# First layer of a two-block kernel: norm by tokens, split input projections, six modulation steps moved

## The chip, the cores and the metric

The program runs on one core of a Trainium2 chip. The metric is the time of one execution in microseconds on the device; lower is better. The core's engines run side by side, each through its own list of instructions, and meet at semaphores: TensorE (PE, its weight loads are shown apart as PEld), VectorE (DVE), ScalarE (ACT), GpSimd (POOL) and SyncE (SP), which issues nearly all large transfers. TensorE adds its results into 8 banks of PSUM.

## What is computed

Two blocks run one after the other on 256 tokens of width 1024, in fp32. The change touches only layer 0 of the first block:

```python
sh1_l, sc1_l, g1_l, sh2_l, sc2_l, g2_l = jnp.split(jax.nn.silu(c) @ ada_w[i] + ada_b[i], 6, axis=-1)
hl = modulate(rms_norm(xl, norm_mix[i]), sh1_l, sc1_l)      # h * (1 + scale) + shift
...  # hc the same way from xc = ctx and c_ctx, where a layer reads the context
yl, yc = even_mixer(hl, hc, ev_w_in[j], ...)                # layer 0
xl = xl + g1_l[:, None] * yl
hl2 = modulate(rms_norm(xl, norm_ffn[i]), sh2_l, sc2_l)
xl = xl + g2_l[:, None] * expert_choice_ffn(hl2, router[i], w_gate[i], w_up[i], w_down[i])
```

`ada_w` is 2 x 1024 x 6144: both layers take their shifts, scales and gates from a product of the condition vector with it. `even_mixer` projects both streams (`h @ w_in`: q, k, v, z, gates and the input of the pooling), runs q, k and v through a convolution of three taps and SiLU, normalizes q and k, runs a gated delta rule over chunks of 64 tokens in both directions (the context gives the start state), pools the pooling input in windows of 2, 4, 8 and 16 along rows of 64 tokens, and multiplies the sum by `w_out`. Then come 16 experts of width 512, each on the 32 tokens that it chooses. Layer 1 has a short convolution in place of the mixer and experts again. The second block isn't touched.

## The kernel before

`build` writes the program of every engine by hand, one function for each, so the order in the code is the order on the engine. PE fills banks in turn: `v_open`/`v_close` a bank of the four that DVE empties, `s_open`/`s_close` one of the four for ACT; on the other side `take` waits for the next filled bank and `drained` gives it back.

**Weights.** `stream` lists chunks of 2 MB (1024 rows by 512 columns). SP loads them in that order into `weight_ring`, four slots for the first 31 chunks; `free_slot` makes SP wait until the chunk that was in the slot has been used (`released`). The stream begins with four chunks of `ada_w`, five of `ev_w_in` (qkv in three, z, pool), the other twenty of `ada_w`, two of `ev_w_out`. Behind them come the experts' chunks of layer 0, in more slots.

**Modulation.** One chunk of `ada_w` is one step: `ada_turn` turns the copied result of the step before with four transposes (through `transposes`, L532) for DVE's `ada_bias`, which sums it and adds the bias; `ada_mm` multiplies the next chunk, 8 matmuls of 32 x 512 (L579), and ACT copies its bank in `ada_copy` (L1470). Each layer has 12 steps. Four come in the head, since the first norm needs them; the others are entries `"ada"` in the list of `mixer_steps`, by which PE, DVE, ACT and POOL all build the mixer. Its pieces there are the rows of decay (`rows`), products of keys, the inverse of each chunk's triangle by levels (`turn`, `grow`, `flip`), `solve` and `kdec` for each head, and `walk`, the pass over the chunks (`state`, `w`, `out`), once for each direction.

**Head.** PE transposes x and ctx (16 banks, L558 and L562), ACT squares the transposed form (L1455 and L1456), `norm_part` sums the squares over features with eight 512-wide matmuls against ones (L596), ACT and DVE make the reciprocal root, DVE scales (L1819, 16 operations of 256 columns) and ACT adds the shift (L1431).

**Projections.** `project` multiplies a chunk in plain fp32 (L636), four quarters of 128 output columns, each over 8 tiles of features. The first qkv chunk and z and pool have 256 columns (x alone), the other two qkv chunks 512 (x and ctx). Behind each quarter ACT copies the bank (L1506 for qkv) and DVE does the convolution. Between z and pool stand the gates' product (`l2_sum` and the gate matmuls, L671 and L678) and the gates' transposes. DVE pools a quarter as it comes (L1975 and the lines behind it), with reciprocal counts made there (L1985). ACT has the Ln/Exp pairs of the l2 norms (L1530, L1532) there.

**The split form.** The rest of the kernel multiplies in `product`: input and weights are each split into a high part (ACT's copy into a shorter type, L1395 for weights, in `high`) and the remainder (DVE's subtraction in `split`, through the helper L1816), and three matmuls (L652 to L654) go over each tile: high by high, low by high, high by low. There are two buffers for the parts of a quarter's weights; `high` waits for the quarter two back to be multiplied.

## Time and profile before

| | us |
|---|---|
| median of 3 runs | 1449.2 |
| lowest and highest | 1444.81 and 1453.25 |
| the profiled execution | 1447.19 |
| its span, first to last instruction | 1445.5 |
| TensorE busy (matmuls) in it | 1212.5 (84%) |
| VectorE, ScalarE, GpSimd busy | 583.4, 413.3, 78.1 |
| mean granted clock of TensorE | 0.928 |

The shares are averages over stages with different limits, so the stages have to be read one by one. PEclk and the clock are shares of TensorE's full speed. A matmul's row gives its duration from start to a modelled end; neighbouring ones overlap, so the distance between two starts is what one costs. "x16" is a run of sixteen instructions. "idle before <-releaser" tells how long the engine had stood idle and which work ended that.

### The profile page before, as it was taken

Reading aid. Unit: us, or ns where it says so; the run is one execution under the profiler, and the core shown is the slowest. Engines: PE = TensorE matmul, PEld = TensorE weight load, DVE = VectorE, ACT = ScalarE, POOL = GpSimd, SP = SyncE. Lnnn points to the kernel's source line nnn. Section 1 sums busy time; section 2 is a strip of 40 time slices with the busy share of each in tenths; the row PEclk is TensorE's granted clock in tenths of the full one; section 3 lists DMA queues with packets and bytes.
Section 4 is the critical chain, followed back from the end, with each engine's and each line's share of the span. In section 5 each row is a group of like instructions: output and inputs, shape, how many; then the busy total and the mean of one; then the engine's idle time right before and its main releaser. Section 6 shows DMA issues by size and latency. Waiting matters only on the chain.

```text
span 1445.5 us, 19111 instructions
## 1 busy us (share of the span) xinstructions
PE 1212.5 (84%) x8105; PEld 873.1 (60%) x8105; DVE 583.4 (40%) x1076; ACT 413.3 (29%) x751; POOL 78.1 (5%) x118
## 2 busy tenths in 40 slices
PE   5899889998986566589998655658899999999887
PEld 2646658785952122159986212115899878899756
DVE  1432684544530000036653000002796366545574
ACT  2323433222310000024332000001454555343562
POOL 4000023430000000000000000000000000010000
PEclk9999999999998788799999988888999999999998
DMA  8713374349589999993547999999243403444000
GB/s 300 292 58 117 127 249 150 117 165 378 203 323 409 409 409 409 409 385 118 186 183 298 410 409 409 409 409 391 94 166 129 147 29 117 175 142 173 36 1 30
DMA packets 125097, 338.63 MB, mean 234 GB/s; under 512 B 8657, under 2 KB 11590, under 8 KB 125014
## 3 DMA queue, kind: packets, MB, share of 16 engines
q1 hardware_dynamic: 117536, 334.51, 60.8%
q10 hardware_dynamic: 7478, 2.91, 0.8%
q8 instruction: 65, 1.06, 0.3%
q14 instruction: 18, 0.15, 0.0%
HBM read 336.35 MB, written 1.05 MB: 233 GB/s over the span
## 4 chain that ended last, share of the span: by engine, by line
PE 62%; DMA 20%; DVE 8%; SPq 6%; ACT 3%; issue 1%; ACTq 0%; DVEq 0%
PE bank L652 9%; PE bank L654 9%; PE bank L653 8%; DMA weight_ring<-in_w_up_dram 7%; PE bank L636 6%; SPq L1220 5%; PE bank L940 4%; DMA weight_ring<-in_w_gate_dram 3%; DVE arena L1816 3%; PE bank L579 2%; PE bank L1104 2%; PE bank L596 2%; DMA weight_ring<-in_w_down_dram 2%; DMA expert_slots<-in_w_down_dram 2%; DMA expert_slots<-in_w_up_dram 2%; SPq L1225 2%
## 5 line engine op out<-in xcount | busy, mean ns | idle before, releaser
L652 PE MATMUL bank<-input_high,weights_high 128*128 128x256 f32 (+1 forms) x992 | 291.7, 294 | 6.6 <-DVE input_low L1816 6.6
L654 PE MATMUL bank<-input_high,weights_low 128*128 128x256 f32 (+1 forms) x992 | 285.0, 287 | 0.0
L653 PE MATMUL bank<-input_low,weights_high 128*128 128x256 f32 (+1 forms) x992 | 284.9, 287 | 0.0
L1816 DVE TENSOR_TENSOR weights_low<-weight_ring,weights_high 128x1024 fp32r<-128x1024 f32 x124 | 151.7, 1224 | 147.0 <-ACT weights_high L1395 146.7
L652 PEld LDWEIGHTS bank<-input_high,weights_high 128*128 128x128 f32 x992 | 189.5, 191 | 11.3 <-issue 8.2
L654 PEld LDWEIGHTS bank<-input_high,weights_low 128*128 128x128 f32 x992 | 189.7, 191 | 0.0
L653 PEld LDWEIGHTS bank<-input_low,weights_high 128*128 128x128 f32 x992 | 189.2, 191 | 0.7
L1395 ACT ACTIVATE weights_high<-weight_ring 128x1024 fp32r<-128x1024 f32 x124 | 130.8, 1056 | 149.6 <-PE bank L654 146.0
L1816 DVE TENSOR_TENSOR arena<-arena,bank 128x512 f32<-128x512 f32 (+1 forms) x38 | 24.8, 652 | 276.1 <-PE bank L940 246.0
L940 PE MATMUL bank<-weight_ring,arena 128*32 128x512 f32 x512 | 77.1, 739 | 55.7 <-DMA weight_ring<-in_w_up_dram 38.2
L636 PE MATMUL bank<-arena,weight_ring 128*128 128x256 f32 (+1 forms) x320 | 98.4, 470 | 2.9 <-DMA weight_ring<-in_ev_w_in_dram 2.9
L636 PEld LDWEIGHTS bank<-arena,weight_ring 128*128 128x128 f32 x320 | 61.8, 194 | 39.2 <-issue 30.6
L940 PEld LDWEIGHTS bank<-weight_ring,arena 128*32 128x32 f32 x512 | 17.3, 126 | 111.6 <-issue 46.7
L1816 DVE TENSOR_TENSOR arena<-arena 128x256 f32<-128x256 f32 (+12 forms) x111 | 60.4, 551 | 27.0 <-ACT arena L1675 9.8
L940 PE MATMUL bank<-expert_slots,arena 128*32 128x512 f32 x256 | 40.6, 770 | 32.8 <-DMA expert_slots<-in_w_gate_dram 22.8
L965 PE MATMUL bank<-weight_ring,arena 128*32 128x512 f32 x256 | 39.3, 749 | 27.4 <-DMA weight_ring<-in_w_down_dram 25.2
L540 PE MATMUL bank<-upper_then_ones 128*128 128x272 f32 x238 | 62.1, 417 | 0.0
L1819 DVE SCALAR_TENSOR_TENSOR arena<-arena,vectors 128x272 f32<-128x272 f32 (+2 forms) x106 | 57.0, 541 | 3.8
L596 PE MATMUL bank<-arena,upper_then_ones 128*128 128x256 f32 (+2 forms) x112 | 41.3, 464 | 16.6 <-ACT arena L1437 12.0
L540 PEld LDWEIGHTS bank<-upper_then_ones 128*128 128x128 f32 x238 | 47.3, 202 | 9.8
L2163 DVE COPY arena<-bank 128x512 f32<-128x512 f32 x8 | 5.5, 691 | 114.7 <-PE bank L965 114.7
L1437 ACT ACTIVATE arena<-residual 128x256 f32<-128x256 f32 (+1 forms) x48 | 20.0, 419 | 109.4 <-DVE residual L1819 63.2
(401 smaller groups left out, 1596.0 us busy)
## 6 DMA issues: line engine op xcount, KB each, us to landing
weight_ring<-in_ada_w_dram SPq DMA_DIRECT2D x24, 2048.0 KB, 8.1
weight_ring<-in_w_gate_dram SPq DMA_DIRECT2D x16, 2048.0 KB, 21.2
weight_ring<-in_w_down_dram SPq DMA_DIRECT2D x16, 2048.0 KB, 21.4
weight_ring<-in_w_up_dram SPq DMA_DIRECT2D x16, 2048.0 KB, 24.4
weight_ring<-in_even_w_in_dram SPq DMA_DIRECT2D x9, 2048.0 KB, 8.8
arena<-in_w_up_dram SPq DMA_DIRECT2D x8, 2048.0 KB, 20.7
expert_slots<-in_w_up_dram SPq DMA_DIRECT2D x8, 2048.0 KB, 24.0
arena<-in_w_gate_dram SPq DMA_DIRECT2D x8, 2048.0 KB, 23.7
```

What stands on the lines that cost most here:

```text
L540: pe.matmul(b[:, 0:L2], ONES, WIDE[:, :], start=True, stop=True)
L596: mm = pe.matmul(b[:, 0:width], ONES, sq[:, k, 0:width], start=k == 0, stop=k == KD - 1 and i != 4)
L636: mm = pe.matmul(b[:, 0:width], w[:, k, m * P:m * P + P], rhs_of(k), start=k == 0, stop=k == KD - 1)
L652: pe.matmul(b[:, 0:width], hi[:, k, :], XHI[:, k, t0:t0 + width], start=k == 0, stop=False)
L653: pe.matmul(b[:, 0:width], hi[:, k, :], XLO[:, k, t0:t0 + width], start=False, stop=False)
L654: mm = pe.matmul(b[:, 0:width], lo[:, k, :], XHI[:, k, t0:t0 + width], start=False, stop=k == KD - 1)
L940: mm = pe.matmul(b[32 * e:32 * e + 32, :], XG[:, 2 * q + k, 32 * e:32 * e + 32], w[:, e, k, :], start=q == 0 and k == 0, stop=q == 3 and k ...
L965: mm = pe.matmul(b[32 * e:32 * e + 32, :], HT[:, f, 32 * e:32 * e + 32], w[:, e, 512 * half:512 * half + 512], start=f == 0, stop=f == 3)
L1220: sp.dma_start(dst.rearrange("p (e n) -> p e n", e=EG), w[e0:e0 + EG, 2 * q * P:(2 * q + 2) * P, :].rearrange("e (p k) n -> p e (k n)", p=P))\
L1395: act.activation(WHI[:, j % 2], chunk(cn)[:, :, m * P:m * P + P], ACT.Copy).then_inc(weights_high, 1)
L1816: return dve.tensor_tensor(out_, a, b, op)
L1819: return dve.scalar_tensor_tensor(out_, a, s, b, op0, op1)
```

## The change

**Norm.** x and ctx are squared and summed along a token's row by ACT as they come from memory (tokens on partitions), four operations of 1024 columns. The reciprocal root is one small value a token; DVE multiplies the rows by it, PE transposes the scaled rows behind the first two modulation products and the first turn, DVE and ACT copy them. The eight ones-products of the head go, the transposes of unscaled ctx too; those of unscaled x stay (the residual needs them).

**Split projections.** DVE applies gain and shift in one operation a tile (`first_scale`), ACT makes the high part, DVE the low part, and `first_product` multiplies the five chunks of `ev_w_in` in three passes. ACT and DVE get a `high` and a `split` for each quarter.

**Six modulation steps** move: one behind each of the qkv chunks and one behind each of the first three pool quarters. Their chunks move in the stream to where they are used. In `mixer_steps` six entries go: the one by the rows of head 1, two in the levels of the backward direction, the one behind the last `solve`, and two of the five in the last `walk`.

**GpSimd.** The index ramps of the pooling come early, and DVE makes the reciprocal counts in the head; the mask `ROW_OF` is made behind `gam_args`.

```diff
@@ -101,7 +101,7 @@
-        if i in (1, 3):
+        if i == 3:
@@ -124,12 +124,12 @@
-            if (lv, slot) in ((LEVELS[0], 2), (LEVELS[1], 1), (LEVELS[2], 3), (LEVELS[2], 4)):
+            if (lv, slot) in ((LEVELS[0], 2), (LEVELS[2], 3)):
                 steps += ada
     for h in range(HEADS):
-        steps += [("solve", 1, h, 0), ("kdec", 1, h, 0)] + (ada if h % 2 else [])
+        steps += [("solve", 1, h, 0), ("kdec", 1, h, 0)] + (ada if h == 1 else [])
     for i, piece in enumerate(walk(1)):
-        steps += piece + (ada if i < 4 or i == 6 else []) + ([("poolmix", 1, i, 0)] if i < 4 else [])
+        steps += piece + (ada if i in (0, 2, 6) else []) + ([("poolmix", 1, i, 0)] if i < 4 else [])
     steps += [("onorm", 1, 0, 3)]
     return steps
@@ -417,13 +421,21 @@
-        stream += [cols(ev, 0), cols(ev, 512), cols(ev, 1024), cols(ev, QKV), cols(ev, QKV + 512 + 16)]
-        W_ADA = len(stream)
-        stream += [cols(ada_w[0], 512 * i) for i in range(4, 12)] + [cols(ada_w[1], 512 * i) for i in range(12)]
+        ada_at = [0, 1, 2, 3]
+        W_EV = []
+        for src, adas in (((ev, 0), 1), ((ev, 512), 1), ((ev, 1024), 1), ((ev, QKV), 0), ((ev, QKV + 512 + 16), 3)):
+            W_EV.append(len(stream))
+            stream += [cols(*src)]
+            for _ in range(adas):
+                ada_at.append(len(stream))
+                stream += [ada_src[len(ada_at) - 1]]
+        for i in range(len(ada_at), 24):
+            ada_at.append(len(stream))
+            stream += [ada_src[i]]
@@ -601,15 +608,20 @@
-            for k in range(KD):
-                norm_part(0, k, 512, SQ1)
-            for i in range(4):
-                if i == 3:
-                    pe.wait_ge(vector_drained, mark[("mod", 0)])
+            ada_mm()
+            ada_mm()
+            pe.wait_ge(scalar_drained, ada["copied"] - 1)
+            ada_turn()
+            for tt in range(2 * TT):
+                pe.wait_ge(tokens_ready, tt + 1)
+                for kh in range(2):
+                    b = s_open() if tt % 2 else v_open()
+                    mm = transposes(b, [(b[:, k * P:k * P + P], XN[:, tt, (4 * kh + k) * P:(4 * kh + k + 1) * P]) for k in range(4)])
+                    (s_close if tt % 2 else v_close)(mm, ("tokens", tt))
+            for i in range(2):
                 ada_mm()
-                if i >= 1:
-                    pe.wait_ge(scalar_drained, ada["copied"] - 1)
-                    ada_turn()
+                pe.wait_ge(scalar_drained, ada["copied"] - 1)
+                ada_turn()
             pe.wait_ge(scalar_drained, ada["copied"])
             ada_turn()
@@ -624,18 +636,33 @@
-            def project(cn, mt, rhs_of, width, opener, closer, names, norm=None):
-
-                arrive(cn)
-                w = chunk(cn)
+            def ada_step():
+
+                if ada["turned"] < ada["next"]:
+                    pe.wait_ge(scalar_drained, ada["copied"])
+                    ada_turn()
+                ada_mm()
+
+            def first_product(i, mt, width, opener, closer, names, between=None):
+
+
+                cn = W_EV[i]
                 for m in range(4):
+                    j = len(quarters)
+                    pe.wait_ge(weights_split, j + 1)
                     b = opener()
+                    hi, lo = WHI[:, j % 2], WLO[:, j % 2]
                     for k in range(KD):
-                        if norm is not None and m == 0:
-                            pe.wait_ge(h_ready, h_count(norm, k + 1))
-                        mm = pe.matmul(b[:, 0:width], w[:, k, m * P:m * P + P], rhs_of(k), start=k == 0, stop=k == KD - 1)
-                    closer(mm, (names, mt + m))
-                released[cn] = (scalar_filled, n["s"]) if closer is s_close else (vector_filled, n["v"])
+                        if j in (0, 4):
+                            pe.wait_ge(first_split, KD * (j // 4) + k + 1)
+                        pe.matmul(b[:, 0:width], hi[:, k, :], XHI1[:, k, 0:width], start=k == 0, stop=False)
+                        pe.matmul(b[:, 0:width], hi[:, k, :], XLO1[:, k, 0:width], start=False, stop=False)
+                        mm = pe.matmul(b[:, 0:width], lo[:, k, :], XHI1[:, k, 0:width], start=False, stop=k == KD - 1)
+                    done = closer(mm, (names, mt + m))
+                    quarters.append((cn, m, scalar_filled if closer is s_close else vector_filled, done))
+                    if between is not None and m < 3:
+                        between()
+                released[cn] = (weights_split, len(quarters))
 
             def product(cn, mt, width, opener, closer, names, new_input=False, after=None, t0=0):
@@ -659,10 +686,13 @@
-            project(W_EV, 0, lambda k: hT[:, k, 0:T], T, s_open, s_close, "qkv", norm=0)
-            project(W_EV + 1, 4, lambda k: hT[:, k, :], 2 * T, s_open, s_close, "qkv")
-            project(W_EV + 2, 8, lambda k: hT[:, k, :], 2 * T, s_open, s_close, "qkv")
-            project(W_EV + 3, 0, lambda k: hT[:, k, 0:T], T, s_open, s_close, "z")
+            first_product(0, 0, T, s_open, s_close, "qkv")
+            ada_step()
+            first_product(1, 4, 2 * T, s_open, s_close, "qkv")
+            ada_step()
+            first_product(2, 8, 2 * T, s_open, s_close, "qkv")
+            ada_step()
+            first_product(3, 0, T, s_open, s_close, "z")
@@ -682,7 +712,8 @@
-            project(W_EV + 4, 0, lambda k: hT[:, k, 0:T], T, v_open, v_close, "pool")
+            first_product(4, 0, T, v_open, v_close, "pool", between=ada_step)
+            mark[("split", -1)] = len(quarters)
@@ -1450,17 +1475,20 @@
-            act.wait_ge(vector_drained, mark["x"])
-            act.wait_ge(scalar_drained, n["s"])
-            act.activation(SQ1[:, :, 0:T], XH[:, :, META:L2], ACT.Square)
-            act.activation(SQ1[:, :, T:2 * T], XC, ACT.Square).then_inc(squares_ready, 1)
+            act.wait_ge(x_in, 16)
+            for t in range(2 * TT):
+                if t == TT:
+                    act.wait_ge(ctx_in, 16)
+                ins = act.activation(at(1024 * t, 1024), XIN[:, t, :], ACT.Square, accum_out=tsum[:, t:t + 1])
+            ins.then_inc(squares_ready, 1)
+            act.wait_ge(squares_ready, 1)
+            then(act.activation(trs, tsum, ACT.Ln, bias=EPSC, scale=1.0 / D))
+            act.activation(trs, trs, ACT.Exp, scale=-0.5).then_inc(rstd_ready, 1)
@@ -1470,12 +1498,26 @@
-                shift(hT[:, k, 0:T], MOD[:, 0, k, 0:1], True)
-                shift(hT[:, k, T:2 * T], MOD[:, 0, k, 1:2], False).then_inc(h_ready, 1)
+            ada_copy()
+            ada_copy()
+            for tt in (1, 3):
+                for kh in range(2):
+                    b = take()
+                    drained(act.activation(hT[:, 4 * kh:4 * kh + 4, tt * P:tt * P + P], bank(b, 4, P), ACT.Copy))
+            ada_copy()
...
+
+            def first_high(c0, signal):
+
+                for k in range(KD):
+                    scaled_tiles[0] += 1
+                    act.wait_ge(h_scaled, scaled_tiles[0])
+                    act.activation(XHI1[:, k, c0:c0 + T], hT[:, k, c0:c0 + T], ACT.Copy).then_inc(signal, 1)
+
+            first_high(0, h_ready)
+            high()
+            high()
+            first_high(T, context_high)
@@ -1504,12 +1546,17 @@
-                if t >= 1:
-                    silu_qkv(t - 1)
-            silu_qkv(11)
+                high()
+                if t % 4 == 3:
+                    ada_copy()
+                if t >= 3:
+                    silu_qkv(t - 3)
             for m in range(4):
                 b = take()
                 drained(act.activation(Z1[:, m, :], b[:, 0:T], ACT.Silu))
+                high()
+                if m < 3:
+                    silu_qkv(9 + m)
 
             b = take()
             drained(act.activation(GPART, b[:, :], ACT.Copy))
@@ -1522,6 +1569,12 @@
+                    high()
+                    ada_copy()
+                    high()
+                    ada_copy()
+                    ada_copy()
+                    n["segment"] += 1
@@ -1918,24 +1976,62 @@
-            for i in range(4):
+            roots[0] += 1
+            dve.wait_ge(rstd_ready, roots[0])
+            then(negated_half(tsum, tnv))
+            then(tt(tnt, trs, trs, MUL))
+            then(tt(tnt, tnt, tnv, MUL))
+            then(stt(trs, tnt, 1.5, trs, ADD, MUL))
+            for t_ in range(2 * TT):
+                dve.tensor_scalar(XN[:, t_, :], XIN[:, t_, :], trs[:, t_:t_ + 1], None, MUL).then_inc(tokens_ready, 1)
+            ada_bias()
+            for t_ in (0, 2):
+                for kh in range(2):
+                    b = take()
+                    drained(dve.tensor_copy(hT[:, 4 * kh:4 * kh + 4, t_ * P:t_ * P + P], bank(b, 4, P)))
...
-            for k in range(KD):
-                stt(hT[:, k, 0:T], XH[:, k, META:L2], gain[:, k, 0:1], NR1[:, 0:T], MUL, MUL)
-                stt(hT[:, k, T:2 * T], XC[:, k, :], gain[:, k, 1:2], NR1[:, T:2 * T], MUL, MUL).then_inc(h_scaled, 1)
+            dve.wait_ge(vector_drained, n["v"])
+            dve.wait_ge(scalar_drained, mark[("tokens", 3)])
+
+            def first_scale(k, r):
+
+                h = hT[:, k, r * T:r * T + T]
+                dve.tensor_scalar(h, h, gain[:, k, r:r + 1], MOD[:, 0, k, r:r + 1], MUL, ADD).then_inc(h_scaled, 1)
+
+            def first_low(k, r, signal, count):
+
+                t0 = r * T
+                dve.wait_ge(signal, count)
+                tt(XLO1[:, k, t0:t0 + T], hT[:, k, t0:t0 + T], XHI1[:, k, t0:t0 + T].bitcast(F32), SUB).then_inc(first_split, 1)
+
+            def first_parts(r, signal, behind):
+
+                for k in range(KD + 2):
+                    if k < KD:
+                        first_scale(k, r)
+                    if k >= 2:
+                        first_low(k - 2, r, signal, k - 1)
+                        if k - 1 in behind:
+                            split()
+
+            first_parts(0, h_ready, (KD,))
+            split()
+            dve.memset(CB[:, :, :, 0:1], 0.0)
+            dve.memset(CB[:, :, :, T + 1:T + 2], 0.0).then_inc(edges_ready, 1)
+            first_parts(1, context_high, (KD,))
+            split()
             vec_copies((1, 2))
             tt(gain_sq, vec("norm_final", 0, 8), vec("norm_final", 0, 8), MUL)
-            dve.memset(CB[:, :, :, 0:1], 0.0)
-            dve.memset(CB[:, :, :, T + 1:T + 2], 0.0).then_inc(edges_ready, 1)
             dve.memset(PADP, 0.0)
 
@@ -1944,6 +2040,10 @@
+                if t in (6, 10):
+                    ada_bias()
+            split()
+            split()
 
@@ -1968,8 +2068,10 @@
-            dve.wait_ge(iota_ready, 4)
             for g in range(4):
+                if g:
+                    ada_bias()
+                split()
@@ -1980,9 +2082,6 @@
-                i0, i1 = IOT[:, 0, 64 * g:64 * g + 64], IOT[:, 1, 64 * g:64 * g + 64]
-                then(stt(i0, i0, float(2 << g), i1, MIN, MIN))
-                then(dve.reciprocal(RCNT[:, g, :], i0))
```

How PE's list stands in the head (`ident,arena` are transposes, L596 the ones-products, L579 and after the change L586 the modulation products, L532 and L544 the helper of the transposes), before:

```order
L558 MATMUL bank<-ident,arena 128x128 x4
L562 MATMUL bank<-ident,arena 128x128 x4
L596 MATMUL bank<-arena,upper_then_ones 128x512 x8
L579 MATMUL bank<-weight_ring,silu_c 32x512 x16
L532 MATMUL bank<-ident,ada_partials 128x128 x4
L579 MATMUL bank<-weight_ring,silu_c 32x512 x8
L532 MATMUL bank<-ident,ada_partials 128x128 x4
L579 MATMUL bank<-weight_ring,silu_c 32x512 x8
L532 MATMUL bank<-ident,ada_partials 128x128 x8
L620 MATMUL bank<-ident,arena 128x16 x8
```

and after:

```order
L558 MATMUL bank<-ident,arena 128x128
L570 MATMUL bank<-ident,arena 128x128 x16
L586 MATMUL bank<-weight_ring,silu_c 32x512 x16
L544 MATMUL bank<-ident,ada_partials 128x128 x4
L544 MATMUL bank<-ident,arena 128x128 x32
L586 MATMUL bank<-weight_ring,silu_c 32x512 x8
L544 MATMUL bank<-ident,ada_partials 128x128 x4
L586 MATMUL bank<-weight_ring,silu_c 32x512 x8
L544 MATMUL bank<-ident,ada_partials 128x128 x8
L632 MATMUL bank<-ident,arena 128x16 x8
```

The eight products of L596 are gone, and 32 transposes of scaled rows stand between the second and the third modulation product, where ctx stood with x ahead of all of them.

ACT's list at the gates, from the third of the four Ln/Exp pairs of 512 columns (L1530, L1532) to the three small exponentials behind `gam_args` (L1527), before, with bank numbers:

```order
L1530 ACTIVATE arena<-bank5,small 128x512
L1532 ACTIVATE arena<-arena 128x512
L1530 ACTIVATE arena<-bank6,small 128x512
L1532 ACTIVATE arena<-arena 128x512
L1527 ACTIVATE small<-small 128x32 x3
```

and after (L1583 and L1585 are the pairs, L1425 the weights' high part, L1498 the modulation copies, L1580 the exponentials):

```order
L1583 ACTIVATE arena<-bank7,small 128x512
L1585 ACTIVATE arena<-arena 128x512
L1583 ACTIVATE arena<-bank4,small 128x512
L1585 ACTIVATE arena<-arena 128x512
L1425 ACTIVATE weights_high_49<-weight_ring 128x1024
L1498 ACTIVATE ada_partials<-bank5 128x512
L1425 ACTIVATE weights_high_49<-weight_ring 128x1024
L1498 ACTIVATE ada_partials<-bank6 128x512
L1498 ACTIVATE ada_partials<-bank7 128x512
L1580 ACTIVATE small<-small 128x32 x3
```

The last two high parts of the pool quarters and three modulation copies stand behind the four pairs now.

## Rows read from the trace of the kernel before

**Rows 1.** Windows: stretch, length, busy us by engine, PEclk, DMA share, GB/s.

```profile
49.00:133.00 84.00, 84.00 (x256) 49.54 (x256) 21.82 (x37) 17.21 (x35) 1.08 (x8) 0.98 0.37 133
217.00:336.00 119.00, 113.36 (x946) 93.42 (x946) 59.15 (x117) 34.63 (x58) 44.11 (x39) 0.98 0.47 166
391.00:632.00 241.00, 164.84 (x1070) 69.38 (x1068) 29.52 (x67) 17.61 (x34) 0.00 (x0) 0.84 1.00 396
```

**Rows 2.** Chain that ended last, in order of time: start, us, what.

```profile
21.17 8.80 PE bank L596 x16
...
31.89 16.93 DMA weight_ring<-in_ev_w_in_dram
48.86 84.40 PE bank L636 x256
...
321.04 1.85 PE bank L579 x16
...
336.21 15.79 DMA weight_ring<-in_ev_w_out_dram
```

**Rows 3.** DMA issues: the fourth modulation chunk; KB, us to landing.

```profile
weight_ring<-in_ada_w_dram SPq DMA_DIRECT2D x1, 2048.0 KB, 21.8
```

**Rows 4.** Timeline, DVE, first scaling of the head: start, us, what.

```profile
41.22 0.48 DVE L1819 SCALAR_TENSOR_TENSOR arena<-residual,small,arena 128x256 f32<-128x256 f32 x1
```

**Rows 5.** Groups by form, 49 to 133 us: busy, mean ns, idle before.

```profile
L1944 DVE TENSOR_SCALAR arena<-arena,vectors 128x256 f32<-128x256 f32 x4 | 1.4, 353 | 11.2 <-ACT arena L1506 11.2
```

**Rows 6.** Timeline: operations of the split form in other stages.

```profile
364.71 2.77 DVE L1816 TENSOR_TENSOR input_low<-arena,input_high 128x256 fp32r<-128x256 f32 x8
...
700.37 1.06 ACT L1395 ACTIVATE weights_high<-weight_ring 128x1024 fp32r<-128x1024 f32 x1 [1.74 <-PE bank L654]
701.99 1.22 DVE L1816 TENSOR_TENSOR weights_low<-weight_ring,weights_high 128x1024 fp32r<-128x1024 f32 x1
703.36 1.06 ACT L1395 ACTIVATE weights_high<-weight_ring 128x1024 fp32r<-128x1024 f32 x1 [1.94 <-PE bank L654]
```

**Rows 7.** Timeline, ACT: copies of projection quarters.

```profile
64.55 0.39 ACT L1506 ACTIVATE arena<-bank 128x256 f32<-128x256 f32 x1 [2.77 <-PE bank L636]
...
71.42 0.60 ACT L1506 ACTIVATE arena<-bank 128x512 f32<-128x512 f32 x1 [6.18 <-PE bank L636]
...
78.28 0.60 ACT L1506 ACTIVATE arena<-bank 128x512 f32<-128x512 f32 x1 [5.97 <-PE bank L636]
```

**Rows 8.** Timeline, PE: decay rows (48 rows in, by head).

```profile
166.36 0.50 PE L722 MATMUL bank<-gamma_rows,direction_head_picks 48*128 48x512 f32 x1 [1.50 <-DVE gamma_rows L1816]
166.79 0.39 PE L723 MATMUL bank<-arena 128*128 128x512 bf16 x1
167.11 0.38 PE L725 MATMUL bank<-gamma_rows,direction_head_picks 48*128 48x256 f32 x1
167.33 0.28 PE L726 MATMUL bank<-gamma_rows,direction_head_picks 48*128 48x256 f32 x1
```

**Rows 9.** Timeline: gates, pooling and the last transposes of this stage.

```profile
138.58 0.60 PE L532 MATMUL bank<-ident,arena 128*128 128x128 f32 x4
...
142.86 0.42 DVE L1975 COPY arena<-bank 128x256 f32<-128x256 f32 x1
...
143.84 0.22 DVE L1819 SCALAR_TENSOR_TENSOR arena<-arena 128x64 f32<-128x64 f32 x1
...
144.68 1.49 DVE L1816 TENSOR_TENSOR arena<-arena 128x256 f32<-128x256 f32 x3
...
145.55 0.63 ACT L1532 ACTIVATE arena<-arena 128x512 f32<-128x512 f32 x1
...
159.71 0.63 PE L699 MATMUL bank<-ident,arena 128*128 128x128 f32 x4 [3.00 <-DVE small L1816]
```

**Rows 10.** Timeline: the last walk and the output product's first split.

```profile
333.89 0.69 DVE L1816 TENSOR_TENSOR arena<-backward_direction,bank 128x512 f32<-128x512 f32 x1 [0.34 <-PE bank L823]
...
352.08 2.00 ACT L1395 ACTIVATE weights_high<-weight_ring 128x1024 fp32r<-128x1024 f32 x2 [3.55 <-DMA weight_ring<-in_ev_w_out_dram]
```

89 lines of the change are left out of this document (44 added, 45 removed).

## The prediction, made before the changed kernel was run

> **What bounds the kernel now.** I read the table of windows first [rows 1]. In the projections (49 to 133 us) TensorE is busy all 84.00 us, DVE 21.82, ACT 17.21, at a DMA share of 0.37: TensorE alone sets this stage. In the mixer (217 to 336 us) it has 113.36 of 119 us. From 391 us on the DMA share is 1.00 over 241 us. The chain of waits says what ends last in the head: the ones-products of the norm (L596), then the first chunk of `ev_w_in`, asked for at 31.89 and there at 48.8 us, then 84.4 us of products [rows 2]. Behind the layer the loads of the experts' chunks stand in SP's order behind the output product's splits, and then the DMA engines are full: a layer that ends earlier starts them earlier, and what is won before 391 us reaches the end.
>
> **The head.** The eight 512-wide norm products go (8.80 us, [rows 2]); ACT now sums squares along a token's row. The modulation products wait for their weights only. The fourth chunk, issued at 12.14 us, lands 21.8 us later, at 33.9 [rows 3]; a product (1.85, [rows 2]), two turns and the copy between them, with hand-overs some 3 us, put the first scaling near 38.9 where it stood at 41.22 [rows 4]. Before, 16 two-input operations followed, of 0.48 us in the row. Now the x half is 8 scalings of the kind that takes 0.353 us at 256 columns [rows 5] and 8 low parts (8 in 2.77 us, [rows 6]), 5.6 us, and behind them in DVE's order the first weight split, 1.22 us [rows 6]: first product near 45.7, 3.2 us early. The first `ev_w_in` chunk can be asked for near 19 us, when the first modulation product has freed its slot; behind two more chunks it lands near 40 and is hidden. If the small transfers of ACT's queue slow it, up to 3 us of this are lost.
>
> **The first four quarters.** Before they took 48.86 to 64.55, 1.9 us more than four of the steady ones [rows 2, 7]. After: quarters 0 and 1 from 45.7 to 51.5 at 2.9 us (1.9 more if the clock is low at their start, as before). Quarter 2 waits: its split is behind DVE's context half (47.0 + 5.6), its high part behind ACT's context parts, which DVE paces, and the copy of quarter 0: 52.6 + 0.39 + 1.06 + 1.22 gives 55.3 [rows 6, 7]. With quarters 2 and 3 and one modulation step of 2.3 us the 512-wide part starts near 63.0 instead of 64.55: 1.6 us won, one step already done.
>
> **The products.** A plain quarter of 512 columns takes 6.86 us (71.42 to 78.28, [rows 7]); of 256 columns (84.4 - 8 x 6.86 - 1.9) / 8 = 3.45. The split form at 256 columns runs in the second layer with quarters 3.0 us apart (ACT's high parts at 700.37 and 703.36), of which 0.1 is DVE's split, ended at 703.21, coming late [rows 6]; I take 2.95, which leaves 0.12 a pass. The disputed price is the split form at 512 columns, which the trace has only once, with 48 rows: L722 lasts 0.50 us where L725, the same form at 256 columns and also behind a change of weights, lasts 0.38, and L726 without that change 0.28; the bf16 product of 512 columns (L723) lasts 0.39 [rows 8]. The step from 256 to 512 columns is thus 0.11 us. On top of 0.12 a pass this makes 0.23 and 5.5 us a quarter. The upper bound is the whole 0.43 us between the starts of L722 and L723, 10.3 us a quarter; the lower one is L723's 0.39 less what L726's 0.28 holds beyond its pass (0.17), 0.217. I take 0.23, since the 0.43 hold a load of another type. Eight quarters: 8 x (6.86 - 5.5) = 10.9 us. Four z quarters: 4 x 0.5 = 2.0. Two more modulation steps lie between, 4.6 us. At the gate product TensorE is 1.6 + 10.9 + 2.0 - 4.6 = 9.9 us ahead, three steps done. What each quarter adds, 1.06 us on ACT and 1.22 on DVE [rows 6], is 17 and 20 us on top of 17.21 and 21.82: hidden at 512 columns; at 256 the loop of copy, high part and split, 0.39 + 1.06 + 1.22 = 2.67 plus hand-overs, is just under a quarter.
>
> On a 512-column pass the Trainium skill, "TensorE: Matmul & The Clock Gate", section "Back-to-back issue gap", gives N/2.4 + 2.5 ns, 216 ns. By that the eight quarters would give 2.4 us more; no K=128 row here shows it, and at 256 columns the trace (0.12) is above that formula's 109 ns.
>
> **Gates and pooling.** Before, from the gate transposes (138.58) to the product that waits for DVE's `gam_args` work (159.71) it takes 21.1 us; DVE reached the first pool group at 142.86, 4.3 us after the transposes, and the rest took 16.85 [rows 9]. Now its first split of this stage comes before that group, and ACT's high part for it stands behind the four Ln/Exp pairs, which ended at 146.2 before, 7.6 us after the transposes [rows 9]: 7.6 + 1.06 + 1.22 = 9.9 instead of 4.3. The four pairs of L1819 and L1985 leave, 0.84 us each (143.84 to 144.68), 3.4 us; one more split (1.22) and three bias steps (two small operations each, of at most the 0.22 us of the smallest row here: 0.4) come in. 9.9 + 16.85 - 3.4 + 1.2 + 1.1 = 25.7, so 4.5 us longer; 1 if ACT is through earlier, 7.5 if the pool products, which now stand a split and a modulation step apart, come late. The three modulation steps between them are done in its shade. At 160 us TensorE is 9.9 - 4.5 = 5.4 us ahead with all six steps done.
>
> **The six steps that left the mixer.** A step is four transposes (0.60 as a row, [rows 9], with the last one's tail under the next instruction: 0.45) and a product (1.85, [rows 2]), 2.3 us. The one behind head 1 hides some of ACT's work: 2.0. Three in the backward direction's levels and solves lie where TensorE is full: 6.9, at least 4.5 if they cover DVE. Two in the last walk cover DVE's 0.69 us [rows 10] between a state and the next product: 3.8, at least 2. Together 12.7, range 8 to 14.
>
> **The tail.** ACT waits 3.55 us for `ev_w_out`, which was asked for at 336.21 and took 15.79 us behind four modulation chunks [rows 2, 10]. Its slot now comes free at the step behind head 1 of `solve`, some 15 us earlier against the walk. That gives 3.4 us; what is late next is ACT's Ln/Exp chain itself. Zero if the transfer is still late.
>
> **Sum.** 5.4 + 12.7 + 3.4 = 21.5 us off the profiled execution's 1447.2 us (span 1445.5 and 1.7 outside): **1426 us**. The median of the runs shown is 1449.2, 2.0 above the profiled one.
>
> **Rivals.** (a) *Cover was worth more than the step.* The removed steps hid DVE and ACT waits, the tail stays late, pooling pays its upper bound: 21.5 - 3.0 - 4.7 - 3.4 = 10.4 us, 1437. For it: all pieces of the walks wait for DVE. Against: TensorE is 95% busy in the levels.
> (b) *The 512-wide pass is slow*, the 0.43 us of L722's spacing: 8 x (10.3 - 5.5) = 38 us more in quarters 4 to 11, 1464 us, slower than before. It decides from 0.34 a pass on (0.23 + 21.5 / 192). For it: all eight L722 are spaced so. Against: the durations of L722, L725, L726 and L723 fit together with half of it.
> (c) *Between*, 0.32 a pass, the spacing less a load: 17 us given back, 1443.
> (d) *Everything at its better bound*: warm clock at the first product, 0.217 a pass, 2 us in pooling: 21.5 + 1.9 + 2.5 + 2 = 27.9 us, 1419.
>
> **Chances.** Forecast 0.67 (own range 1419 to 1433, from the bounds above), (a) 0.15, (b) 0.05, (c) 0.05, (d) 0.08. The range 1416 to 1440 takes in all but (b), (c) and part of the edges. 0.5%, about what a measurement of this kernel can tell from no change, is 7.2 us. Faster by more: the forecast, (a) and (d), less a small part of (a), 0.89; within 0.5%: (c) and that part, under 0.06, say 0.05; slower 0.06.
>
> **What would show it.** Passes of L658 to L660 at 512 columns 0.22 to 0.24 us apart; first product near 45.7 us and a wait of `weights_low` before the third quarter; gate product near 123 us; in pooling DVE waiting for `weights_high`; no wait of ACT for `ev_w_out`; the output product near 343 instead of 365 us. Passes 0.3 us or more apart, or a mixer that keeps its length with six steps fewer, would make the number wrong.

## The result, and the profile after

The changed kernel takes 1442.2 us in the median of 20 runs (1434.7 to 1449.9), the kernel before 1449.1 (1439.9 to 1457.5): a ratio of 0.9944, with a 95% interval of 0.9922 to 0.9966. It is faster, by 7 us and not by 23, and 2 us outside the range. On the chip of the first experiments the same pair gave 0.9895 (0.9868 to 0.9922), so the gain is known to a few us only; the positions of the stages, below, repeat better.

The profiled execution took 1444.9 us, its span 1443.2. The windows that answer to [rows 1] (stretch, length, busy us by engine with instructions, PEclk, DMA share, GB/s; the projections up to the gates' product, the mixer's middle, the experts):

```profile
48.07:128.24 80.17, 76.94 (x440) 62.88 (x440) 47.03 (x78) 36.77 (x64) 0.00 (x0) 0.98 0.62 219
217.00:336.00 119.00, 110.02 (x908) 93.81 (x908) 61.24 (x117) 34.01 (x57) 44.78 (x39) 0.97 0.40 139
379.00:620.00 241.00, 174.61 (x1056) 74.17 (x1058) 29.18 (x66) 16.40 (x32) 0.00 (x0) 0.77 0.99 396
```

The projections take 80 us instead of 84, three modulation products included; TensorE is still the engine that works through them (76.94 of 80.17), with DVE and ACT twice as busy as in [rows 1] beside it. The experts are as full of transfers as before.

Where the stages stand, in us from the start of the span, read from the timelines of TensorE:

| | before | before again | after | after again | row_late | best1 |
|---|---|---|---|---|---|---|
| first product | 48.9 | 49.2 | 48.1 | 48.0 | 47.9 | 46.1 |
| gates' product | 133.2 | 132.0 | 128.2 | 128.2 | 126.0 | 124.0 |
| v's last transposes end | 160.3 | 159.6 | 159.9 | 159.8 | 157.8 | 155.6 |
| first decay rows | 166.4 | 165.7 | 167.0 | 166.9 | 163.8 | 161.8 |
| first chain product | 188.0 | 187.3 | 188.8 | 188.7 | 181.6 | 182.7 |
| last walk's first state | 328.9 | 328.3 | 324.9 | 324.8 | 317.0 | 316.0 |
| output product | 365.3 | 364.8 | 353.2 | 353.1 | 346.9 | 344.3 |
| layer 0's experts, last gate or up product | 611.8 | 611.0 | 599.5 | 599.5 | 596.8 | 592.1 |
| second block's first product | 1030.8 | 1027.1 | 1021.7 | 1018.8 | 1013.3 | 1011.2 |
| end | 1445.5 | 1445.1 | 1443.2 | 1436.2 | 1431.2 | 1426.1 |

Up to the output product two executions of one kernel agree within 0.7 us (within 1.2 at the gates), and there the change is worth 12.1 us. All of it is still there at the end of the first experts (12.3). Behind that it is 9.1 at the second block and 2.3 at the end in this pair of profiles, 8.3 and 8.9 in the other.

The parts of the forecast can be read one by one. Copies of two neighbouring 512-wide quarters on ACT, as in [rows 7]:

```profile
71.95 0.60 ACT L1548 ACTIVATE arena<-bank 128x512 f32<-128x512 f32 x1 [3.43 <-PE bank L660]
...
77.56 0.60 ACT L1548 ACTIVATE arena<-bank 128x512 f32<-128x512 f32 x1 [3.75 <-PE bank L660]
```

A quarter takes 5.61 us where it took 6.86: 0.234 us a pass, where I had 0.23 and feared 0.43. The Trainium skill, "TensorE: Matmul & The Clock Gate", section "Back-to-back issue gap", gives 216 ns at full clock as the gap of a 512-column matmul by itself, and 131 ns sustained in a stream with weight loads. The trace has such a stream and is 8% above the first figure and far above the second, so the measurement decides. At 256 columns 24 passes take 2.88 us, 0.120 each.

Two holes of TensorE (its timeline: start, us, what, idle before and who ended it), ahead of the third quarter and of the first decay rows:

```profile
56.79 0.58 PE L658 MATMUL bank<-first_input_high,weights_high 128*128 128x256 f32 x1 [2.83 <-DVE weights_low L1869]
...
167.00 0.79 PE L750 MATMUL bank<-gamma_rows,direction_head_picks 48*128 48x512 f32 x1 [3.90 <-DVE gamma_rows L1869]
```

The second row stood at 166.36 with 1.50 us of idle time and 0.50 of duration in [rows 8]. The duration tells the clock: behind both holes TensorE runs at half of it. Windows of 5 us, after:

```profile
160.00:165.00 5.00, 3.03 (x24) 1.17 (x24) 5.00 (x6) 3.91 (x10) 4.28 (x2) 1.00 1.06 390
165.00:170.00 5.00, 3.00 (x6) 1.28 (x6) 1.84 (x7) 1.64 (x7) 0.00 (x0) 0.60 1.04 381
170.00:175.00 5.00, 5.00 (x21) 4.12 (x20) 0.69 (x1) 2.86 (x10) 0.00 (x0) 0.50 1.05 387
175.00:180.00 5.00, 5.00 (x27) 3.24 (x27) 2.63 (x6) 2.88 (x10) 1.50 (x2) 0.88 0.28 104
```

A granted clock of 0.50 is 1.2 GHz of 2.4. What DVE did in the second hole, and GpSimd beside it (DVE's timeline, then GpSimd's):

```profile
161.63 4.06 DVE L1872 SCALAR_TENSOR_TENSOR arena<-arena 128x256 f32<-128x256 f32 x4
...
166.26 0.68 DVE L1869 TENSOR_TENSOR gamma_rows<-bank,gamma_rows 16x512 fp32r<-16x512 f32 x1
```

```profile
159.38 1.80 POOL L1350 MEMSET backward_direction<- 128x2048 f32 x1 [144.26 <-DVE small L1869]
161.69 3.10 POOL L1300 TENSOR_SCALAR_AFFINE_SELECT backward_direction<-backward_direction 128x2048 f32<-128x2048 f32 x1 [0.50 <-POOL backward_direction L1350]
```

Four scalings, each of which reads two inputs from SBUF and takes 0.41 us, took 4.06 together: one of them, begun at 161.97, lasted 3.06 us and ended at 165.03, as GpSimd's select ended at 164.79. That select is the mask `ROW_OF`, which the change moved behind `gam_args`. In the kernel before, the same select ran from 13.15 to 16.03 us, beside copies of DVE out of a bank (one input, none from SBUF), which took their 0.69 us.

### The profile page after: what moved, and what is told of

The parts are those of the page before. It is cut to its first block, busy times and chain, and to the rows that moved or that the text cites. A ratio compares the mean times of both kernels' runs of the same rounds, so it can differ in the third digit from the quotient of the medians.

```text
span 1443.2 us, 19524 instructions
## 1 busy us (share of the span) xinstructions
PE 1225.7 (85%) x8265; PEld 896.7 (62%) x8265; DVE 616.7 (43%) x1120; ACT 432.4 (30%) x777; POOL 78.2 (5%) x118
## 4 chain that ended last, share of the span: by engine, by line
PE 63%; DMA 17%; DVE 10%; SPq 4%; ACT 3%; issue 2%; ACTq 1%; DVEq 0%
PE bank L679 9%; PE bank L681 9%; PE bank L680 9%; DMA weight_ring<-in_w_up_dram 7%; PE bank L968 4%; DMA expert_slots<-in_w_down_dram 3%; DMA arena<-in_w_up_dram 3%; DMA weight_ring<-in_w_down_dram 3%; DVE arena L1869 3%; PE bank L993 2%; SPq L1248 2%; PE bank L586 2%; PE bank L1132 2%; PE bank L891 2%; PE bank L947 2%
## 5 line engine op out<-in xcount | busy, mean ns | idle before, releaser
L1869 DVE TENSOR_TENSOR weights_low<-weight_ring,weights_high 128x1024 fp32r<-128x1024 f32 x144 | 176.1, 1224 | 185.2 <-ACT weights_high L1425 184.8
L679 PEld LDWEIGHTS bank<-input_high,weights_high 128*128 128x128 f32 x992 | 189.6, 191 | 13.4 <-issue 10.6
L1425 ACT ACTIVATE weights_high<-weight_ring 128x1024 fp32r<-128x1024 f32 x144 | 151.7, 1055 | 146.4 <-PE bank L681 146.1
L968 PE MATMUL bank<-weight_ring,arena 128*32 128x512 f32 x512 | 83.7, 796 | 45.9 <-DMA weight_ring<-in_w_up_dram 33.2
L968 PE MATMUL bank<-expert_slots,arena 128*32 128x512 f32 x256 | 45.5, 850 | 28.2 <-DMA expert_slots<-in_w_gate_dram 17.7
L1869 DVE TENSOR_TENSOR arena<-arena 128x256 f32<-128x256 f32 (+14 forms) x107 | 57.7, 546 | 26.3 <-ACT arena L1728 9.8
L993 PE MATMUL bank<-weight_ring,arena 128*32 128x512 f32 x256 | 42.4, 799 | 25.2 <-DMA weight_ring<-in_w_down_dram 23.5
L658 PE MATMUL bank<-first_input_high,weights_high 128*128 128x256 f32 (+1 forms) x160 | 54.1, 338 | 5.6 <-DVE weights_low L1869 5.6
L586 PE MATMUL bank<-weight_ring,silu_c 128*32 128x512 f32 x384 | 49.2, 633 | 7.2 <-DMA weight_ring<-in_ada_w_dram 7.2
L659 PE MATMUL bank<-first_input_low,weights_high 128*128 128x256 f32 (+1 forms) x160 | 53.4, 333 | 0.0
L660 PE MATMUL bank<-first_input_high,weights_low 128*128 128x256 f32 (+1 forms) x160 | 52.6, 329 | 0.0
```

The lines of the kernel that those rows point to most:

```text
L586: mm = pe.matmul(b[j:j + 32, :], CS[:, 2 * k:2 * k + 32], w[:, k, :], start=k < 4, stop=k >= 4)
L658: pe.matmul(b[:, 0:width], hi[:, k, :], XHI1[:, k, 0:width], start=k == 0, stop=False)
L659: pe.matmul(b[:, 0:width], hi[:, k, :], XLO1[:, k, 0:width], start=False, stop=False)
L679: pe.matmul(b[:, 0:width], hi[:, k, :], XHI[:, k, t0:t0 + width], start=k == 0, stop=False)
L968: mm = pe.matmul(b[32 * e:32 * e + 32, :], XG[:, 2 * q + k, 32 * e:32 * e + 32], w[:, e, k, :], start=q == 0 and k == 0, stop=q == 3 and k ...
L993: mm = pe.matmul(b[32 * e:32 * e + 32, :], HT[:, f, 32 * e:32 * e + 32], w[:, e, 512 * half:512 * half + 512], start=f == 0, stop=f == 3)
```

## Experiments

**Twice the same: before_again, after_again.** No edit.

> The kernel before, unchanged: a second profiled execution beside the first, to see how far the positions of its stages move by themselves. In the first one TensorE's output product of the first layer began at 365.3 us and the second block's first product at 1030.8, and 414.6 us lay from there to the end. Theory A (what the changed kernel lost behind the second block's first product, 6.8 us in its profile, is the clock's scatter between executions): 414.6 moves by several us here too. Theory B (the change itself lengthens the end): this run repeats 414.6 within 1 us, and the changed kernel repeats 421.5.

> The changed kernel, unchanged: a second profiled execution. Up to the output product (353.2 us in the first) both theories expect the same within about 2 us. From the second block's first product to the end the first profile had 421.5 us at a granted clock of 0.94: theory A (scatter) expects another length here, 413 to 422; theory B (the change lengthens it) 421.5 again.

Measured: from the second block's first product to the end 418.0 us (before: 414.6 in the first profile), and 417.4 for the changed kernel (421.5 in the first). Both kernels lie in one band, 414.6 to 421.8 over all profiles of this study. One kernel moves by 3.4 and 4.1 us between its two executions. Theory A holds: the instructions are the same, and the granted clock differs, as these windows of after and of after_again show.

```profile
1021.70:1443.20 421.50, 401.53 (x2860) 360.77 (x2860) 250.63 (x398) 199.54 (x347) 6.46 (x11) 0.93 0.30 103
```

```profile
1018.80:1436.20 417.40, 397.10 (x2860) 356.41 (x2860) 250.45 (x398) 199.53 (x347) 6.44 (x11) 0.95 0.30 104
```

In time, before_again gave 0.9972 against the kernel before, that is itself, with an interval that just misses 1 (0.9998): differences of 0.3% between kernels mean nothing here.

**The mask later: row_late.**

```diff
-            pool.wait_ge(gam_args, 1)
+            pool.wait_ge(vector_drained, mark["gamma_rows"])
             then(pool.memset(ROW_OF, 0.0))
```

> One wait changed: GpSimd makes the mask ROW_OF (a 128x2048 memset and a select of the same size, 1.8 and 3.1 us) behind the drained gamma rows instead of behind gam_args. Theory C (DVE's l2 scaling that took 3.06 us instead of 0.41 stood still because GpSimd's select ran beside it): the four scalings take 0.41 each again, the gamma rows come 2.5 us earlier, the hole of TensorE ahead of the first decay rows shrinks from 3.9 to 1.3 us, and the stage at half clock behind it becomes shorter; the output product begins 2.5 to 7 us earlier than 353. Rival (the 3.06 us were a wait for ACT's reciprocal roots): nothing moves, since ACT's roots are where they were.

DVE's scalings, and TensorE's first decay rows behind them, in row_late:

```profile
159.40 1.09 DVE L1872 SCALAR_TENSOR_TENSOR arena<-arena 128x256 f32<-128x256 f32 x3
160.86 0.42 DVE L1872 SCALAR_TENSOR_TENSOR arena<-arena 128x256 f32<-128x256 f32 x1 [0.38 <-ACT arena L1585]
```

```profile
163.77 0.49 PE L750 MATMUL bank<-gamma_rows,direction_head_picks 48*128 48x512 f32 x1 [1.50 <-DVE gamma_rows L1869]
```

Measured: the scalings take 0.41 us each again, the hole is 1.50 us instead of 3.90, and the clock is 1.00 from 161 to 208 us. From v's last transposes to the decay rows it takes 5.9 us instead of 7.1 (with a half clock at 157 to 161 us in this execution), from there to the first chain product 17.8 instead of 21.8. That is 5.2 us in this execution, 1.2 before the rows and 4.0 of clock behind them (the first product's quarters, which fell otherwise under the clock, gave 2.1 more by chance; of the 7.2 us ahead at the chain product 6.2 are left at the output product). Output product at 346.9, time 1433.1 us against 1436.3 for after_again on the same chip, four runs each, which can't be told apart. Theory C is confirmed for the stretched scaling and the hole. The 4.0 us of clock are not steady: the other runs with the late mask had nearly the same hole and mostly fell to half clock behind it.

| us | hole | v's last transposes to the decay rows | from there to the chain product | half clock that began in the hole or behind it |
|---|---|---|---|---|
| before (one modulation step more) | 1.50 | 6.0 | 21.6 | 3.4 |
| after, after_again, small_late | 3.90 | 7.1 | 21.8 | 10.2 |
| row_late | 1.50 | 5.9 | 17.8 | none |
| high_early | 1.80 | 5.0 | 19.4 | 3.4 |
| cover_step | 1.80 | 5.0 | 20.8 | 6.8 |
| best1 | 1.50 | 6.2 | 20.8 | 6.8 |

Over both stretches the late mask gave 1.9 (best1) to 5.2 us (row_late). Two windows from the decay rows to the chain product, row_late and best1:

```profile
163.77:181.58 17.81, 17.81 (x114) 11.91 (x114) 10.17 (x19) 12.92 (x43) 9.33 (x6) 1.00 0.64 228
```

```profile
161.84:182.66 20.82, 20.81 (x115) 14.09 (x115) 10.14 (x19) 13.18 (x43) 9.33 (x6) 0.84 0.55 193
```

The rule for the stretched scaling is in the Trainium skill, "SBUF — State Buffer", section "Who interferes with whom": a DVE instruction with two inputs in SBUF and a GpSimd instruction that reads SBUF exclude each other for a whole instruction, one that only writes doesn't take part. This trace agrees in the first half: the select stopped the scaling until it ended. The second half is not shown here: beside GpSimd's memset (159.38 to 161.18) DVE made only copies out of banks, and no run has a scaling beside a memset of this size.

**The small loads later: small_late.**

```diff
-            for dst, src in small_src:
-                act.dma_start(dst, src, allow_slow_non_contiguous=True).then_inc(small_in, 16)
...
                 if t >= 3:
                     silu_qkv(t - 3)
+                for dst, src in {4: small_src[0:5], 5: small_src[5:6], 6: small_src[6:]}.get(t, []):
+                    act.dma_start(dst, src, allow_slow_non_contiguous=True).then_inc(small_in, 16)
```

> ACT issues the seven small loads (gates' weights, biases, ssd_d) between the 512-wide quarters instead of in the head, and takes the two small exponentials with the gates. Theory D (ACT stood in its DMA issues until 27.4 us, which delayed the first modulation copy, the turn behind it and with it the transposes of the scaled tokens, so that the third and fourth modulation products came 2 us after their weights): first scaling near 39 us instead of 41.0, first product near 46 instead of 48.1, gate product 2 us earlier. Rival (the weights' loads set the head): the fourth chunk still lands near 34.3 and the first scaling stays within 0.5 us of 41.

The first modulation copy on ACT's timeline, after and then small_late:

```profile
23.76 3.64 ACTq L1491 DMA_DIRECT2D small<-in_ssd_d_dram  x2
27.44 0.60 ACT L1498 ACTIVATE ada_partials<-bank 128x512 f32<-128x512 f32 x1 [13.40 <-issue]
```

```profile
20.47 0.60 ACT L1496 ACTIVATE ada_partials<-bank 128x512 f32<-128x512 f32 x1 [6.23 <-issue]
...
39.62 1.06 ACT L1513 ACTIVATE first_input_high<-arena 128x256 fp32r<-128x256 f32 x3 [1.97 <-DVE arena L2004]
```

Measured: first scaling at 39.2 us instead of 41.0, first product at 46.2 instead of 48.0, output product at 351.9, 1.2 us earlier. Theory D holds: the queue of DMA issues on ACT (two of them 3.64 us) held the copy for which the turn, and behind it on TensorE the transposes of all tokens and two modulation products, waited. The fourth chunk landed at 34.4 us, as before. The time is that of after_again (1437.2 against 1436.3): the profile lost what it had won under a half clock between output product and experts (57.3 us there instead of 53.9).

**Plain matmuls: plain_form.** ACT and DVE make the parts, TensorE multiplies chunk by input in one plain matmul.

```diff
-                        pe.matmul(b[:, 0:width], hi[:, k, :], XHI1[:, k, 0:width], start=k == 0, stop=False)
-                        pe.matmul(b[:, 0:width], hi[:, k, :], XLO1[:, k, 0:width], start=False, stop=False)
-                        mm = pe.matmul(b[:, 0:width], lo[:, k, :], XHI1[:, k, 0:width], start=False, stop=k == KD - 1)
+                        mm = pe.matmul(b[:, 0:width], chunk(cn)[:, k, m * P:m * P + P], hT[:, k, 0:width], start=k == 0, stop=k == KD - 1)
```

> The changed kernel with the three matmuls of a tile replaced by one plain fp32 matmul of the same chunk and the same input; ACT and DVE still make all split parts. Theory E (TensorE's passes set the projections, 5.60 us a 512-wide quarter split against 6.87 plain, 2.88 against 3.45 at 256 columns): quarters of 6.87 and 3.45 us again, gate product 8 x 1.27 + 8 x 0.57 = 15 us later, near 143 us, and the output product 15 to 17 us later than 353. Rival (the splitting on ACT and DVE sets them, or the clock pays the gain back): the gate product moves by less than 8 us.

Neighbouring copies of 512-wide quarters in plain_form:

```profile
80.50 0.60 ACT L1546 ACTIVATE arena<-bank 128x512 f32<-128x512 f32 x1 [5.02 <-PE bank L658]
...
87.37 0.60 ACT L1546 ACTIVATE arena<-bank 128x512 f32<-128x512 f32 x1 [5.02 <-PE bank L658]
```

Measured: 6.87 us a quarter, gates' product at 140.4 (12.2 later; the 15 had counted four quarters that wait for DVE anyway), output product at 369.2, 16.1 later. The time is 1458.5 us, 1.0044 of before (1.0019 to 1.0070). Theory E holds: the three passes in place of the plain matmul are worth 16 us at the output product, more than the whole change (12.1). The rest of the change costs 4 us. ACT and DVE still make the split parts here, so what these cost (the wait before the third quarter, the longer pooling) lies in that rest, with the mask.

**The steps back: steps_back.** On row_late; `mixer_steps` as before, `ada_step`, `ada_copy` and `ada_bias` out of the projections.

```diff
-            ada_step()
             first_product(1, 4, 2 * T, s_open, s_close, "qkv")
-            ada_step()
...
-            first_product(4, 0, T, v_open, v_close, "pool", between=ada_step)
+            first_product(4, 0, T, v_open, v_close, "pool")
```

> row_late with the six modulation steps back in the mixer where they stood before, none between the projections, and the stream in that order. Theory F (a step costs TensorE about 2.4 us wherever it stands, save where it covers a wait; what the move gains is the tail, where ev_w_out's slot comes free earlier): gate product 7 us earlier than row_late's 126.0, last transposes of v about 5 us earlier than 157.8 since DVE then sets that stage, and the output product 3 to 6 us later than row_late's 346.9. Rival (the move gave nothing): the output product within 1.5 us of 346.9.

TensorE in steps_back, a pool quarter without a step ahead of it, and ahead of the output product:

```profile
136.59 0.58 PE L658 MATMUL bank<-first_input_high,weights_high 128*128 128x256 f32 x1 [3.59 <-DVE weights_low L1861]
...
353.06 1.49 PE L771 MATMUL bank<-arena,upper_then_ones 128*128 128x512 f32 x2 [4.59 <-ACT arena L1630]
```

Measured: gates' product at 121.3 (4.8 earlier), v's last transposes at 151.6 (6.2 earlier), and the output product at 359.6, 12.7 us later than row_late's. Theory F had the sign, but a quarter to a half of the size. In the pooling stage the three steps cost 1.5 us together, since without them TensorE waits 3.59 us for a split and works at half clock behind it. In the mixer a step costs its 2.4 us, and at the tail the wait of 4.59 us and a stage at half clock come back (14 us from the last walk's end to the output product, 10 with the steps moved). Moving the steps is worth 12.7 us between these two profiles, a part of which is clock: from decay rows to chain product it takes 23.1 us instead of row_late's 17.8, where one step more explains 2.4. In time it is about half: steps_back takes 1439.3 us, 0.992 of before (0.989 to 0.995), against 0.987 (0.985 to 0.990) for row_late, on another chip.

**A step as a cover: cover_step.** On row_late.

```diff
-            if (lv, slot) in ((LEVELS[0], 2), (LEVELS[2], 3)):
+            if (lv, slot) in ((LEVELS[0], 2),):
...
-        steps += [("solve", 1, h, 0), ("kdec", 1, h, 0)] + (ada if h == 1 else [])
+        steps += [("solve", 1, h, 0), ("kdec", 1, h, 0)] + (ada if h % 2 else [])
```

> row_late with one modulation step moved from the last level of the backward direction back behind the last solve. Theory G (that step covered DVE's copies ahead of the last walk: its removal turned 2.4 us of product into 2.13 us of waiting): the wait of 2.13 us ahead of the first state is gone and the walk's first state comes 2.1 us earlier than row_late's 317.0, everything behind it too. Rival (the wait is for something that the step would only delay): the wait stays and nothing moves.

The last walk's first state in row_late, then in cover_step:

```profile
316.99 1.29 PE L843 MATMUL bank<-backward_direction 128*128 128x128 f32 x8 [2.13 <-DVE backward_direction L2166]
```

```profile
317.28 1.93 PE L586 MATMUL bank<-weight_ring,silu_c 128*32 128x512 f32 x16
319.13 1.16 PE L843 MATMUL bank<-backward_direction 128*128 128x128 f32 x8
```

Measured: the wait is gone. The earlier stages fell otherwise under the clock (v's last transposes 1.9 us later than in row_late), so I compare from the first walk's first state on: to the last walk's it takes 33.0 us instead of 35.3. Theory G holds. The time is 1433.5 us, as row_late's on another chip.

**All three: best1; and one instruction more: high_early.** best1 is row_late, small_late and cover_step in one. high_early moves the third pool quarter's high part up among ACT's pairs:

```diff
+                if i == 2:
+                    high()
                 if i == 4:
-                    high()
                     ada_copy()
```

> All three repairs together: ROW_OF behind the gamma rows, the small loads and exponentials out of the head, the step behind the last solve. If they add: first product near 46, gate product near 124.5, output product near 346.9 - 1.8 - 2.1 = 343 us, and the whole 3 to 8 us faster than the changed kernel. Rival (what is won ahead of the experts is lost to the stage at half clock between output product and experts, which took 57.4 us instead of 53.9 in row_late and small_late): output product near 343, but the experts' first product no earlier than 401.

> best1 with one instruction of ACT moved: the high part of the third pool quarter's weights stands behind the second of the four Ln/Exp pairs of q and k instead of behind the fourth. Theory J (DVE waits 4.4 us for that high part in the pooling stage, and DVE then sets the end of the stage): DVE's split of it comes 2.3 us earlier, the last transposes of v end about 2 us earlier than 155.6 (by TensorE's own work no more than 2), and what follows moves with them. Rival (TensorE sets the stage, its three modulation steps included): the last transposes of v move by less than 0.7 us.

Measured: best1 has its output product at 344.3 and the experts' first product at 399.7. It takes 1427.1 us, 0.984 of before (0.978 to 0.990), 9 us less than after_again took on another chip. The output product stands 1.3 us later than the sum of the single gains had it (343), and a part goes in the stage before the experts (55.4 us instead of 53.9). In high_early DVE waits 1.94 us for that high part instead of 4.4, the stage from gates' product to v's last transposes is 0.8 us shorter (30.9 instead of 31.7), and the decay rows stand 1.3 us earlier. But the gates' product stood 0.8 us later in this execution, so v's last transposes end at 155.6 as in best1: the 2 us of J didn't come, and the rival's number (less than 0.7) did. The wait was real, and TensorE's own work had nearly filled the stage. The output product comes at 341.3, 3.0 us earlier than in best1, 1.5 of it in the stretch behind the decay rows, where the half clock was shorter. The time can't be told from best1's (1428.7).

**Filling the holes: fill_after, fill_best, fill_sized, best2.** Matmuls that nobody reads, ahead of the waits; in fill_sized five ahead of the third quarter and eight ahead of the decay rows, in best2 (on high_early) two and three at v's transposes and the rows:

```diff
+                        b = s_open()
+                        for _ in range(8):
+                            pe.matmul(b[:, 0:L2], ONES, WIDE[:, :], start=True, stop=True)
                         pe.wait_ge(vector_drained, mark["gamma_rows"])
```

> The changed kernel with idle TensorE time filled by matmuls whose result nobody reads: 9 more ahead of the first product, 10 ahead of the third quarter, 7 ahead of the transposes of v, 15 ahead of the first decay rows (0.24 us each). Theory H (TensorE's half clock in 57 to 60 and in 166 to 176 us follows from the holes of 2.8 and 3.9 us before it, and 6 us of what the change wins are given back there): the granted clock stays at 1.00 in both stages, the third quarter takes 3.1 us instead of 4.6, walk 0's first state comes 6 to 7 us earlier than 289.5 and the output product near 346.5. Rival (the clock falls for another cause than idle time): both stages fall to half clock all the same, and nothing moves.

> The same filling on best1, 6 matmuls ahead of the decay rows where the hole is 1.5 us. Theory H: no half clock at 47 to 50 and at 162 to 169 us, walk 0's first state 4 to 5 us earlier than best1's 283.0 and the output product near 340 us instead of 344.3, the whole 2 to 5 us faster than best1. Rival: the clock falls at the same places, output product at 344.

> The changed kernel with filling of the right length: 5 unread matmuls (0.48 us each, 2.4 us) ahead of the third quarter, whose hole is 2.84 us, and 8 (3.8 us) ahead of the first decay rows, whose hole is 3.90 us. Theory H: the granted clock stays at 1.00 behind both, the third quarter takes 3.1 us instead of 4.6, the first decay rows start where they would without it (1.5 us earlier, by the quarter), the stretch from them to the first chain product takes 17.8 us instead of 21.8, and walk 0's first state comes 4 to 5.5 us earlier than 289.5. Rival (filling only moves the fall of the clock to the next hole, at 215 us): the first chain product is 5 us earlier, but the stretch behind it to walk 0 is 2 us or more longer than 100.7.

> high_early (all repairs, and the high part of the third pool quarter moved up) with 2 unread matmuls ahead of the transposes of v and 3 ahead of the decay rows, for its holes of 1.16 and 1.80 us. Theory H: no half clock at 163 to 166 us, the stretch from the first decay rows to the first chain product 17.8 us instead of 19.4, output product near 339.7 instead of 341.3, and the whole within 2 us of high_early and best1, 20 us or so faster than before. Rival: the next hole falls deeper, and the output product stays at 341.

The windows of fill_sized that answer to those of after:

```profile
165.00:170.00 5.00, 4.77 (x26) 2.94 (x25) 1.04 (x3) 2.97 (x12) 0.00 (x0) 1.00 1.05 387
170.00:175.00 5.00, 5.00 (x33) 3.62 (x30) 3.13 (x7) 3.98 (x13) 1.32 (x2) 1.00 1.05 387
```

Measured: in fill_after, fill_best and fill_sized the clock stays at 1.00 behind them, and from decay rows to chain product it takes 17.81 us, as in row_late, against 21.8 of the changed kernel (and 21.6 of before). So the half clock behind the hole of 3.90 us costs 4.0 us. In fill_after and fill_best I had the length wrong (0.48 us a matmul), and the overlong filling cost more than it gave: the output product comes at 357.7 and 348.1 us, later than without it (353.1 and 344.3), and the times are 1445.1 and 1435.0 us. In fill_sized the chain product comes 4.7 us earlier than in after_again, the output product only 2.4 (350.7): part went in the walks, and the time, 0.9928 of before, isn't one that could be told from the changed kernel's. In best2 the clock fell at 163 us all the same, though TensorE's longest idle stretch since 121 us had been 0.41 us (19.4 us from rows to chain, as in high_early): so theory H is shown for the hole of 3.9 us (three executions with it fell, three with filling didn't) and, by fill_after and fill_best alone, for the 2.8 us ahead of the third quarter. In fill_sized the clock had already fallen at the first quarter (48.8 to 52.2 us). Something else than these holes lowers the clock too, and what it is stays open. best2 takes 1425.6 us, 0.985 of before (0.981 to 0.990), and can't be told from best1.

## Why the prediction was wrong

The mechanism of the gain was right and the size was not: 21.5 us were forecast for the output product and all behind it, and 12.1 came there. The steps that failed are three: that the modulation products of the head wait for their weights only, that moving the mask costs nothing, and that the step behind the last `solve` is worth its own length. Term by term:

- **The pass** (the term with the disputed price) was right: 0.234 us instead of 0.23, 5.61 a quarter instead of 5.5. Rivals (b) and (c) are out. Eight quarters, their steps and z took 1.9 us more than in the sum, by 0.1 a quarter and a late split at z.
- **The head** failed: first scaling at 41.0 and not 38.9. I had the fourth chunk's landing right (34.3) and let its product start there. It started at 36.3, since the step "the modulation products wait for their weights only" left out what stands ahead of them in TensorE's order: 32 token transposes, behind a turn, behind a copy on ACT, behind 25 DMA issues. I named ACT's small transfers as a load on the DMA engines, not as time on ACT. 2.1 us, and 2.4 by the first product (48.1 and not 45.7); small_late gives 1.8 of them back.
- **The first four quarters**: 0.7 us more. The wait before the third was forecast, its half clock was counted at the first quarter.
- **Gates and pooling** came out as forecast, 31.7 us against 27.1, 4.5 longer. The steps' shade was there (steps_back), though in the end TensorE's own work and not DVE closed the stage.
- **The mask ROW_OF** isn't in the sum at all. I read it as moved off the head and put no price on the place where it went: beside DVE's two-input scalings on which the decay rows wait. 2.4 us of waiting, and TensorE at half clock for 10 us behind it, where before some 7 us lay at half clock around the shorter hole. At v's last transposes TensorE was 0.4 us ahead of before; by the step behind the fourth head's rows it should have won 2.0 more, by a step left out, and it was 0.8 behind (184.95 against 184.12 us). So 3.3 us of the miss arose here. The late mask gives 0.9 to 2.1 us back ahead of the rows, and 1.9 to 5.2 us with the clock behind them, over the four runs that have it and the same steps.
- **The step behind the last solve** was priced at 2.3 us and was worth 0.1, since it covered DVE (2.13 us of wait). This was rival (a)'s mechanism, but for one of six steps; the two in the levels gave 5.0 (4.6 were forecast) and the two in the walk 3.8, as forecast.
- **The tail** was worth more than its 3.4: last walk's end to output product 10.0 us instead of 14.3.
- **Behind the output product** nothing was forecast. Layer 0's experts kept the gain whole, as the argument of the full DMA engines says. Later stages scatter: from the second block on by 3.4 and 4.1 us between two executions of one kernel, and by 7.2 over all profiles.

Together 5.0 to the gates, 3.3 at the rows, 2.2 at the solve, less 0.4 in the levels and 0.9 at the tail: 9.2, and 21.5 - 9.2 is 12.3, within 0.2 us of what the output product shows. The chance of 0.15 for (a) and the upper bound of the range held no case in which an edit that I had priced at nothing has a price. The median gained 7 us in one set of runs and 17 in another, around these 12; why is not shown, beyond the scatter of the clock.
